# Attention scores of two branches contracted over all 128 rows, and the rotation cut into four pieces

## The reference

```python
for i in range(DEPTH):
    h = rmsnorm(x, norm_g[i])
    proj = h @ w_in[i]                       # one wide projection, cut into all q, k, v, gates
    ya = forgetting_attention(qa, ka, va, logf)                 # 8 heads x 64, no rotation
    qb_rot, ks, kw = rope(qb), rope(ksb), rope(kwb)             # positions rotate q and k
    yb = nsa_attention(qb, qb_rot, ..., ks, vs, kw, vw, gates)  # compressed + selected + window
    yc = differential_attention(rope(qc), rope(kc), vc, lam)    # 4 heads, two 64-wide maps each
    x = x + (gated merge of the three branches) @ w_out[i]      # then the per-layer embedding

def rope(t):                                 # half = 32 of the 64 channels
    return concat([t1 * cos - t2 * sin, t2 * cos + t1 * sin])

s = einsum('qd,kd->qk', q, k) * 64 ** -0.5   # d = 64: the contraction of every score
prob = softmax(where(kpos <= qpos, s, NEG))  # causal: a block of 128 queries sees 128 to 512 keys
```

## Time and profile before

| | |
|---|---|
| median of 3 runs | 1534.54 us (1533.0 to 1534.96) |
| the profiled execution, its own time | 1534.6 us |
| its span | 1532.8 us |
| PE busy | 1498.8 us |
| DVE busy | 935.4 us |
| ACT busy | 634.6 us |
| mean granted PE clock | 0.996 |

### The profile page before, as it was taken

One profiled execution on the slowest core, in us unless ns is written; L12 is line 12 of the kernel. 1 busy time (PEld: TensorE's weight loads), 2 busy tenths in 40 slices (PEclk: granted clock), 3 DMA queues, 4 the chain that ended last, 5 costly groups with the idle time before them and its releaser, 6 DMA issues.

```text
span 1532.8 us, 22548 instructions
## 1 busy us (share of the span) xinstructions
PE 1498.8 (98%) x7957; PEld 1205.8 (79%) x7957; DVE 935.4 (61%) x2197; ACT 634.6 (41%) x1499; POOL 74.4 (5%) x80
## 2 busy tenths in 40 slices
PE   8999999999999999999999999999999999999997
PEld 6778777777787777888787887777887887778885
DVE  6866755555556766454576667655555666755544
ACT  6544433334344444343444334334333444434343
POOL 1000000000000010000100000000000000000011
PEclk9999999999999999999999999999999999999998
DMA  7333332222223332332342334222222233233221
GB/s 197 84 83 90 97 77 63 56 69 62 70 63 96 93 80 83 105 105 70 107 108 69 103 83 117 56 57 62 63 63 76 70 96 89 72 101 100 86 86 72
DMA packets 250301, 129.50 MB, mean 84 GB/s; under 512 B 45690, under 2 KB 245972, under 8 KB 250196
## 3 DMA queue, kind: packets, MB, share of 16 engines
q1 hardware_dynamic: 250196, 128.13, 31.4%
HBM read 118.67 MB, written 2.10 MB: 79 GB/s over the span
## 4 chain that ended last, share of the span: by engine, by line
PE 88%; DVE 6%; ACT 3%; issue 2%; DMA 0%; SPq 0%; ACTq 0%; DVEq 0%
PE D L748 24%; PE D L750 22%; PE D L749 22%; PE Ob L936 7%; PE S L895 5%; PE T L914 4%; DVE w_lo L1304 2%; ACT w_hi L1066 1%; PE Mb L952 1%; ACT probs L1182 1%; DVE v_b L1399 1%; PE Mb L862 1%; PE Ob L940 1%; PE Mb L829 1%; DMA acc<-in_x_dram 0%
## 5 line engine op out<-in xcount | busy, mean ns | idle before, releaser
L748 PE MATMUL D<-h_hi,w_hi 128*128 128x512 f32 x1264 | 544.8, 431 | 4.7 <-DVE w_lo L1304 2.3
L750 PE MATMUL D<-h_lo,w_hi 128*128 128x512 f32 x1264 | 496.4, 393 | 0.0
L749 PE MATMUL D<-h_hi,w_lo 128*128 128x512 f32 x1264 | 494.6, 391 | 0.0
L1304 DVE TENSOR_TENSOR w_lo<-raw,w_hi 128x512 fp32r<-128x512 f32 (+2 forms) x504 | 293.9, 622 | 296.3 <-ACT w_hi L1066 296.1
L1066 ACT ACTIVATE w_hi<-raw 128x512 fp32r<-128x512 f32 (+2 forms) x504 | 263.5, 568 | 292.0 <-PE D L750 289.3
L1182 ACT ACTIVATE probs<-probs,nmax 128x128 f32<-128x128 f32 (+3 forms) x256 | 141.9, 555 | 358.7 <-DVE nmax L1554 358.6
L748 PEld LDWEIGHTS D<-h_hi,w_hi 128*128 128x128 f32 x1264 | 238.5, 189 | 65.4 <-issue 20.6
L750 PEld LDWEIGHTS D<-h_lo,w_hi 128*128 128x128 f32 x1264 | 237.3, 188 | 53.2
L749 PEld LDWEIGHTS D<-h_hi,w_lo 128*128 128x128 f32 x1264 | 239.4, 189 | 30.3 <-issue 0.5
L1554 DVE CUSTOM_DVE_ANT_0 probs<-S,maskb 128x128 f32<-128x128 f32 (+3 forms) x256 | 115.0, 486 | 44.6 <-PE S L895 28.7
L546 DVE COPY pT<-T 128x128 f32<-128x128 f32 (+3 forms) x160 | 77.4, 486 | 60.7 <-PE T L914 59.9
(11 more groups left out here) (245 smaller groups left out, 1495.6 us busy)
## 6 DMA issues: line engine op xcount, KB each, us to landing
raw<-in_w_in_dram SPq DMA_DIRECT2D x124, 512.0 KB, 3.9
raw<-in_w_in_dram SPq DMA_DIRECT2D x32, 256.0 KB, 3.8
raw<-in_w_out_dram SPq DMA_DIRECT2D x16, 512.0 KB, 4.1
raw<-in_w_ple_gate_dram SPq DMA_DIRECT2D x16, 512.0 KB, 4.2
rs<-rx SPq DMA_DIRECT2D x80, 64.0 KB, 2.0
raw<-in_cmp_w_k_dram SPq DMA_DIRECT2D x8, 512.0 KB, 3.7
raw<-in_cmp_w_v_dram SPq DMA_DIRECT2D x8, 512.0 KB, 3.8
raw<-in_w_br_a_dram SPq DMA_DIRECT2D x16, 256.0 KB, 2.9
```

What stands on the lines that cost most here:

```text
L748: pe.matmul(o, w_hi[:, sl, cs], hi[:, k, :], start=(k == 0), stop=False)
L749: pe.matmul(o, w_lo[:, sl, cs], hi[:, k, :], start=False, stop=False)
L750: ins = pe.matmul(o, w_hi[:, sl, cs], lo[:, k, :], start=False, stop=last)
L1304: TT(w_lo[:, sl, half], raw[:, ring(L, t, RAW), half], f(w_hi[:, sl, half]), ALU.subtract).then_inc(M["dve_lo"], 1)
```

## The change

1. **Scores of B and C.** Each head's q is stacked: one half of the partitions holds its high part, the other its low part (`q_st`). Its k is placed in two parts, the low part on both halves and the high part on both halves. A head's score is then two 128-row matmuls, q_st·k_lo and q_st·k_hi: four per `S` where there were six of 64 rows. The product lo·lo comes in as well. Branch A stays as it was. The second head now waits by itself for its bank.
2. **Placing.** The rotated parts no longer land in `arena` directly. ACT writes the high part over `rs`, DVE the low part over `rc`, which now lie side by side in `rcs`, and a new item `put` lets SP copy them to their places: four DMAs, of 64x512 elements for a q, of 64x1024 for a k. The `swap` DMAs of a rotation wait until all earlier puts have landed.
3. **Pieces.** The rotation is now `swap` (with the cosine product on DVE), `rot` (the sum), `high` (ACT) and `low` (DVE), at steps 8, 11, 12, 13; `put` at 13, for kwb at 17. For kc all are two steps sooner.
4. **Third branch's last unit.** `V` follows `T` by two ticks, not one; `Y` stays at its tick.
5. **Stage 3.** kwb, za 3 and vsb change places. `vbd` has memory of its own and is zeroed once at the start by POOL, not in each layer.

```diff
-    st[3] = [("qb", 0), ("w1v", 0), ("kwb", 0), ("w1v", 1), ("za", 3), ("w1v", 2), ("vsb", 0), ("w1v", 3), ("vwb", 0)]
+    st[3] = [("qb", 0), ("w1v", 0), ("vsb", 0), ("w1v", 1), ("kwb", 0), ("w1v", 2), ("za", 3), ("w1v", 3), ("vwb", 0)]
...
-                follow.append([8, ("swap", t)])
-                follow.append([11, ("rot", t)])
+                at = 9 if kind == "kc" else 11
+                follow.append([at - 3, ("swap", t)])
+                follow.append([at, ("rot", t)])
+                follow.append([at + 1, ("high", t)])
+                follow.append([at + 2, ("low", t)])
+                follow.append([17 if kind == "kwb" else at + 2, ("put", t)])
...
-                    vq.append((tick + 1, ti))
+                    vq.append((tick + (2 if u == UNITS - 1 else 1), ti))
...
-                            late.append((tick + (2 if u < UNITS - 1 else 3), ("Y", u)))
+                            late.append((tick + 2, ("Y", u)))
...
+        def places(kind, n):
+            if kind[0] == "q":
+                return [(q_st[n % 2][h][half((h + part_) % 2), :], rcs[half(h), part_ * S:(part_ + 1) * S])
+                        for h in range(2) for part_ in range(2)]
+            at = {"ksb": KS, "kwb": KW, "kc": KC[n % 2]}[kind]
+            return [(part(at + 2 * h, 2)[half(g), :], rcs[half(h), :]) for h in range(2) for g in range(2)]
+
+        def place(M, eng, t):
+            kind, n, _ = tiles[t]
+            eng.wait_ge(M["qk_s"], rots.after(t))
+            if kind == "kwb":
+                eng.wait_ge(M["pe_dense"], tile_of[("w1v", 3)] + 1)
+            elif kind != "ksb":
+                eng.wait_ge(M["pe_s"], rows_before[(4 if kind == "qb" else 8) + n - 1])
+            for dst, src in places(kind, n):
+                eng.dma_start(f(dst), src).then_inc(M["put_s"], 16)
...
                             if n > 1:
-                                sp.wait_ge(M["pool_rot"], n - 1)
+                                sp.wait_ge(M["put_s"], put_before[tiles[it[1]][:2]])
                             for a, b in ((0, 32), (32, 0), (64, 96), (96, 64)):
                                 sp.dma_start(rs[a:a + 32, :], src[b:b + 32, :]).then_inc(M["sw_ld"], 16)
...
+                        if it[0] == "put":
+                            place(M, sp, it[1])
...
-                            for step, (qx, kx) in enumerate(((q_hi[b], ka), (q_lo[b], ka), (q_hi[b], kb))):
-                                last = step == 2 and m != "a"
                                 for h in range(2):
-                                    ps = slice(HD * h, HD * h + HD)
-                                    ins = pe.matmul(Sc[h][:, 0:n], qx[ps, qs], kx[ps, 0:n], start=(step == 0), stop=last)
...
+                            else:
+                                at = {"c": KC[u % 2], "sel": KS, "win": KW}[m]
+                                for h in range(2):
+                                    pe.wait_ge(M["dve_max"], r - 1 + h)
+                                    qx = q_st[b][h][:, qs]
+                                    pe.matmul(Sc[h][:, 0:n], qx, part(at + 2 * h)[:, 0:n], start=True, stop=False)
+                                    pe.matmul(Sc[h][:, 0:n], qx, part(at + 2 * h + 1)[:, 0:n], start=False, stop=True).then_inc(M["pe_s"], 1)
```

More of the change, by code:

```diff
@@ L313, in hybrid_trunk @@
                 hids.add(kind)
-        elif it[0] == "rot":
-            qk_ready.add(tiles[it[1]][:2])
+        elif it[0] == "put":
+            placed.add(tiles[it[1]][:2])
         elif it[0] in ("vt", "gates", "ht", "kcmp", "vcmp", "cs", "ct", "Y"):
@@ L405, in hybrid_trunk, with half @@
         w_lo = sb("w_lo", [P, SPL, 8 * P], F32R)
-        at_arena = -(-nc.sbuf_base // 32) * 32
         arena = sb("arena", [P, 16 * S], F32R)
-        vbd = nc.alloc_sbuf_tensor_at("vbd", [P, 2, P], F32, offset=at_arena + 12 * S * 4)
         def part(n, k=1):
             return arena[:, n * S:(n + k) * S]
-        q_hi, q_lo = [part(0), part(1)], [part(2), part(3)]
-        k_hi, k_lo = [part(4), part(5)], [part(6), part(7)]
-        ks_hi, ks_lo, kw_hi, kw_lo = part(8), part(9), part(10), part(11)
+        def half(h):
+            return slice(HD * h, HD * h + HD)
+        q_hi, q_lo = [part(0), part(2)], [part(1), part(3)]
+        k_hi, k_lo = [part(4), part(6)], [part(5), part(7)]
+        q_st = [[part(2 * b + h) for h in range(2)] for b in range(2)]
+        KC, KS, KW = (4, 8), 8, 12
         flat_both = part(12, 4).rearrange("p (m c) -> p m c", m=16)
@@ L562, in landed_at @@
             return slot_sum[t % RAW] + 16 * ((t - T0) // RAW + 1)
-        def rot_dst(kind, n):
-            if kind == "ksb":
-                return ks_hi, ks_lo, None
-            if kind == "kwb":
-                return kw_hi, kw_lo, None
-            u = (4 if kind == "qb" else 8) + n
-            return (k_hi[u % 2], k_lo[u % 2], u) if kind == "kc" else (q_hi[u % 2], q_lo[u % 2], u)
+        def places(kind, n):
[7 more added lines that the diff above has]
+            eng.wait_ge(M["qk_s"], rots.after(t))
+            if kind == "kwb":
+                eng.wait_ge(M["pe_dense"], tile_of[("w1v", 3)] + 1)
[3 more added lines that the diff above has]
+                eng.dma_start(f(dst), src).then_inc(M["put_s"], 16)
+        put_sum, at_ = {}, 0
+        for x_ in placed.order:
+            at_ += 16 * len(places(*x_))
+            put_sum[x_] = at_
+        put_before = {x_: put_sum[x_] - 16 * len(places(*x_)) for x_ in put_sum}
         with nc.Block() as block:
@@ L898, in _ @@
-                            if m == "a":
-                                for h in range(2):
-                                    ps, hh = slice(HD * h, HD * h + HD), 2 * u + h
+                            if m == "a":
+                                if r >= 2:
+                                    pe.wait_ge(M["dve_max"], r)
+                                for step, (qx, kx) in enumerate(((q_hi, k_hi), (q_lo, k_hi), (q_hi, k_lo))):
+                                    for h in range(2):
+                                        pe.matmul(Sc[h][:, 0:n], qx[b][half(h), qs], kx[b][half(h), 0:n], start=(step == 0), stop=False)
+                                for h in range(2):
+                                    ps, hh = half(h), 2 * u + h
@@ L1167, in _ @@
                             A(lf[:, 3, :], lf[:, 2, :], ACT.Ln, bias=1.0).then_inc(M["act_lf"], 1)
-                        elif what == "rot":
+                        elif what == "high":
                             t = it[1]
                             kind, n, s = tiles[t]
-                            hi_, lo_, u = rot_dst(kind, n)
                             act.wait_ge(M["dve_rs"], rots.after(t))
-                            if u is not None and u >= 2:
-                                act.wait_ge(M["pe_s"], rows_before[u - 1])
-                            A(hi_, rc[:], ACT.Copy).then_inc(M["act_rot"], 1)
+                            A(new_hi, rc[:], ACT.Copy).then_inc(M["act_rot"], 1)
                         elif what == "S":
@@ L1454, in _ @@
                                 STT(zs[:], th[:, slot, :], 1.0, Db[:], ALU.add, ALU.mult).then_inc(done, 1)
-                            elif kind in ROTATED:
-                                r = rots.after(t)
-                                dve.wait_ge(M["act_evac"], act_evac.after(t))
-                                if r > 1:
-                                    dve.wait_ge(M["qk_s"], r - 1)
-                                TT(rc[:], (qf if kind == "qb" else rx)[:], cosT[:], ALU.mult).then_inc(M["dve_rm"], 1)
                             elif kind in ("kcb", "vcb"):
@@ L1542, in _ @@
                             dve.wait_ge(M["dve_rm"], r)
-                            TT(rc[:], rc[:], rb[:], ALU.add).then_inc(M["dve_rs"], 1)
+                            TT(rc[:], rc[:], rs[:], ALU.add).then_inc(M["dve_rs"], 1)
+                        elif what == "swap":
+                            t = it[1]
+                            r = rots.after(t)
+                            dve.wait_ge(M["act_evac"], act_evac.after(t))
+                            if r > 1:
+                                dve.wait_ge(M["put_s"], put_before[tiles[t][:2]])
+                            TT(rc[:], (qf if tiles[t][0] == "qb" else rx)[:], cosT[:], ALU.mult).then_inc(M["dve_rm"], 1)
+                        elif what == "low":
+                            r = rots.after(it[1])
                             dve.wait_ge(M["act_rot"], r)
-                            TT(lo_, rc[:], f(hi_), ALU.subtract).then_inc(M["qk_s"], 1)
+                            TT(new_lo, rc[:], rs[:], ALU.subtract).then_inc(M["qk_s"], 1)
                         elif what == "S":
```

55 lines of the change are left out of this document (23 added, 32 removed).

## The result

The changed kernel takes **1517.59 us** (median of 4 runs, 1516.96 to 1519.57), the kernel before on the same chip 1534.75 (4 runs, 1533.0 to 1535.11): ratio 0.9893, 95% interval 0.9881 to 0.9905. That is 17.2 us faster where 24 were forecast, inside the range of 1503 to 1523 and at the edge of the likeliest case's own range (1504 to 1518).

What follows compares the result with a forecast made beforehand. PE's own work was taken to bound branches B and C. Savings 22.6 + 1.4 + 1.9 - 0.8 - 1.1 = 24.0 us, so 1534.5 - 24.0 = 1510.5 us, range 1503 to 1523.

Steps and rivals of the forecast that it cites:

- the likeliest case: The forecast itself: chance 0.79, its own range 1504 to 1518 us from the bounds of the group prices.
- The bound: Branches B and C: the time is PE's own work; its waits within the change's reach are 2.3 and 1.4 us.
- the edge: Score groups, B and C: 0.4 us at 512 columns lost entering and leaving the 64-row form; gone with 128 rows.
- the group prices: Score groups of B and C at 0.92, 0.70, 0.48 and 0.44 us for 512 to 128 columns: 22.6 us saved.
- The rotation's puts: At each kc in branch C: four puts take 4.0 us, cover and need are equal, PE should see little.
- 0.8 lost: PE's loss where DVE waits for POOL at the 8 places with a kc, 0.1 us a place.
- `zs` in stage 3: Stage 3: with the subtraction behind za 3's evacuation, PE's wait of 0.7 us a layer goes, 1.4 us saved.
- Tail: End of each layer: the last `V`'s 1.12 us stall for `pT` goes, 0.2 comes back at `Y`; 1.9 us saved.
- New small waits: PE reaches its readers sooner, against exponentials and copies no faster: 1.1 us lost in all.
- 1: Score groups: the edge stays, four slots replace three, 15.2 us lost there, 1547 us in all; chance 0.05.
- 2, late puts: Puts at each kc take 8 us instead of 4; PE loses 10 to 20 us, so 1520 to 1530; chance 0.12.
- 3: PE's freed time is waited away on the softmax chain: about 1530 us, at best no difference; chance 0.04.

Runs made afterwards that it cites:

- tail_old: The changed kernel with `V` and `Y` of the last unit back at their old ticks: 1519.38 us, ratio 0.9901.
- after: The changed kernel itself, against the kernel before: 1517.59 us, ratio 0.9893.
- kc_late: The changed kernel with kc's pieces at the same steps as the other tiles', two steps later: 1555.68 us, ratio 1.0139.
- kc8: The changed kernel with kc's pieces one further step sooner (at 8 for 9): 1528.74 us, ratio 0.9965.
- rows64: The changed kernel with the score matmuls of B and C cut to one 64-row half each, half of each contraction left out: 1524.66 us, ratio 0.9930.

## Why the prediction was right, and what it had wrong

- **The bound, the edge, the group prices: right.** PE's own work set the time; 22.3 us saved by the rows, 22.6 forecast; the guess for 384 columns (0.175 a matmul) is 0.18.
- **The rotation's puts: the mechanism seen, the place and the size missed.** "DVE will wait for POOL by 0 to 0.7 us in the 8 places" held in six of them (five without a wait, one of 0.59), the others were 0.74 and 1.71; the put of a q took 4.28 us for 4.0. The step that failed is "I take 4.0 for four puts too", applied to a k, whose put of 1 MB takes 6.8, and asked only where the next *swap* waits for it, not where the next unit's scores do. And I moved POOL's product without asking what stands beside it on DVE. The term "0.8 lost" was 4.8.
- **`zs` in stage 3: wrong sign.** "Nothing else moves there" failed: za 3 moved behind the group of 512 columns, and its evacuation now waits behind a `w_lo` that waits for ACT. 1.4 saved became 0.2 lost.
- **Tail:** 1.9 forecast; the lead grows by 0.1 and 1.5 us there, and tail_old shows 1.1 as the shift's own part.
- **New small waits:** 1.1 allowed, 1.9 missing in branch B, of which 1.1 show as idle time.
- Sum: 22.3 - 4.8 - 0.2 + 1.6 - 1.9 = 17.0; the span fell by 17.1, the median by 17.2.
- **The range** held with some luck. It was drawn from the bounds of the group prices, and those came true to 0.3 us; the 7 us that are missing come from terms that had no bounds.
- **Rivals.** 1 is refuted by two runs. 2, late puts, was right in kind: after loses to it 1.7 us of waits in three places, and far more with the kc steps set otherwise, 38 us at kc_late (beyond the rival's 10 to 20) and 11 at kc8. 3 didn't come. The sum was 7 us too good above all because two of its five terms took a place as quiet that the change itself made busy.

## What to carry to other kernels

Price a matmul form by the distance of starts over its edges, one slot before and behind, not by its slots. When an instruction is moved on POOL, look at what DVE does in that very microsecond, and when one is moved on DVE, look at what it waits for: engines go in order, so a step sooner can cost as much as a step later. A transfer's landing must be checked against every reader, the far one too.

## What the hardware showed that I had not expected

- A VectorE instruction with two SBUF inputs beside a GpSimd product is held until the product ends: `w_lo` 1.78 us for 0.69, a multiply of 6 columns 1.26 for 0.17.
- Four SBUF-to-SBUF DMAs of 128 KB have landed 4.28 us behind the first issue (the next swap's start), four of 256 KB after 6.8 (the reader's start).
- 64-row matmuls on different halves run side by side even when issued in pairs per head (rows64), and going into that form and out costs 0.42 us at 512 columns. The first weight load behind each change of form came with its own matmul, not 0.23 us ahead of it.
- PE idle for 4.04 us brought the granted clock from 1.00 to 0.50 and cost 2.2 us more after the wait was over (kc_late, the same at all six waits).
